# A block of engine programs that ends without GpSimd's drain, in a one-core encoder layer

## The reference

```python
def reference(...):
    for l in range(DEPTH):                      # DEPTH = 1
        xp = mixer_sublayer(xp, ...)            # x + projection of (gated conv, two-way mLSTM)
        xs = mixer_sublayer(xs, ...)
        xp = expert_choice_sublayer(xp, ...)    # 16 experts, each takes its top tokens
        xs = expert_choice_sublayer(xs, ...)
    y_prompt = rms_norm(xp, final_g)
    y_sample = rms_norm(xs, final_g)

def expert_choice_sublayer(x, norm_g, w_router, w_gate, w_up, w_down):
    tokens = rms_norm(x, norm_g).reshape(n_tok, d)
    affinity = softmax(tokens @ w_router)
    gate, idx = lax.top_k(affinity.T, cap)
    xe = tokens[idx]
    hid = silu(xe @ w_gate) * (xe @ w_up)       # per expert
    ye = (hid @ w_down) * gate[..., None]
    out = zeros.at[idx.reshape(-1)].add(ye.reshape(-1, d))
    return x + out
```

## Time and profile before

| | |
|---|---|
| median of three runs | 1306.37 us |
| lowest and highest | 1306.22, 1306.75 us |
| span of the profiled execution | 1307.2 us |
| PE busy in the span | 1253.9 us, 96% |
| POOL busy in the span | 325.7 us, 25% |
| instructions | 25113 |

### The profile page before, as it was taken

One profiled execution on the slowest core, in us unless ns is written; L12 is line 12 of the kernel. 1 busy time (PEld: TensorE's weight loads), 2 busy tenths in 40 slices (PEclk: granted clock), 3 DMA queues, 4 the chain that ended last, 5 costly groups with the idle time before them and its releaser, 6 DMA issues.

```text
span 1307.2 us, 25113 instructions
## 1 busy us (share of the span) xinstructions
PE 1253.9 (96%) x9762; PEld 1029.6 (79%) x9814; DVE 905.7 (69%) x1298; ACT 742.0 (57%) x1079; POOL 325.7 (25%) x316
## 2 busy tenths in 40 slices
PE   7999999999999999779999999999999999999992
PEld 6868986666687888568988898888888888888881
DVE  6462122541586655978888888888888889888985
ACT  7645322222345544447667766776676677667762
POOL 2512221010143231141133213221323132313040
PEclk9999999999999999989999999999999999999996
DMA  8231544361188763388999999999999999999894
GB/s 268 70 116 55 167 140 136 107 180 37 61 256 236 226 211 114 115 312 269 336 305 313 321 334 298 316 324 331 299 310 327 330 298 312 326 331 297 294 372 182
DMA packets 242032, 314.76 MB, mean 241 GB/s; under 512 B 16096, under 2 KB 206048, under 8 KB 241968
## 3 DMA queue, kind: packets, MB, share of 16 engines
q1 hardware_dynamic: 226576, 268.54, 62.2%
q0 software_dynamic: 15392, 45.36, 11.8%
HBM read 274.41 MB, written 39.44 MB: 240 GB/s over the span
## 4 chain that ended last, share of the span: by engine, by line
PE 89%; DMA 4%; DVE 3%; ACT 2%; issue 2%; SPq 1%; POOL 0%; DVEq 0%; ACTq 0%; POOLq 0%
PE psum L2253 23%; PE psum L2114 15%; PE psum L2260 11%; PE psum L2276 8%; PE psum L2081 8%; PE psum L1965 8%; PE psum L2294 4%; PE psum L2285 4%; PE psum L2246 1%; DMA eraw<-in_w_up_dram 1%; PE psum L2027 1%; ACT yt L1248 1%; DMA woraw<-in_w_out_dram 1%; PE psum L1987 1%; PE psum L1945 1%
## 5 line engine op out<-in xcount | busy, mean ns | idle before, releaser
L1812 DVE TENSOR_TENSOR elo<-eraw,ehi 128x2048 bf16<-128x2048 f32 x192 | 433.1, 2283 | 1.0 <-POOLq L822 1.0
L1218 ACT ACTIVATE ehi<-eraw 128x2048 fp32r<-128x2048 f32 x192 | 362.2, 1902 | 25.8 <-PE psum L2294 18.6
L2253 PE MATMUL psum<-xc,ehi 128*128 128x320 f32 x2048 | 332.4, 314 | 1.9 <-DVE xc L1817 1.9
L2253 PEld LDWEIGHTS psum<-xc,ehi 128*128 128x128 f32 x2048 | 304.2, 189 | 3.5 <-DVE xc L1817 2.3
L2260 PE MATMUL psum<-xb,elo 128*128 128x160 bf16 x2048 | 164.4, 234 | 0.0
L1825 DVE TENSOR_REDUCE gu<-psum 128x320 f32<-128x640 f32 x128 | 105.0, 820 | 82.6 <-PE psum L2260 82.5
L2260 PEld LDWEIGHTS psum<-xb,elo 128*128 128x128 bf16 x2048 | 139.0, 98 | 13.2 <-issue 0.2
L2114 PE MATMUL psum<-hn_nar,wnar 128*128 128x512 bf16 (+1 forms) x748 | 141.2, 343 | 1.2
L2276 PE MATMUL psum<-ehi,hc 128*128 128x512 f32 x512 | 132.6, 406 | 0.0
L2114 PEld LDWEIGHTS psum<-hn_nar,wnar 128*128 128x128 bf16 x768 | 73.0, 98 | 63.0 <-issue 4.5
L2276 PEld LDWEIGHTS psum<-ehi,hc 128*128 128x128 f32 x512 | 95.1, 188 | 22.2
(11 more groups left out here) (290 smaller groups left out, 1657.9 us busy)
## 6 DMA issues: line engine op xcount, KB each, us to landing
eraw<-in_w_gate_dram SPq DMA_DIRECT2D x64, 1024.0 KB, 6.3
eraw<-in_w_up_dram SPq DMA_DIRECT2D x64, 1024.0 KB, 8.9
eraw<-in_w_down_dram SPq DMA_DIRECT2D x64, 1024.0 KB, 13.3
wraw<-in_w_in_dram SPq DMA_DIRECT2D x12, 1024.0 KB, 7.5
negm<-negm_d SPq DMA_DIRECT2D x10, 512.0 KB, 7.2
acc_d<-x POOLq DMA_DIRECT2D x10, 512.0 KB, 5.4
tok_d<-tk POOLq DMA_DIRECT2D x10, 512.0 KB, 2.9
v<-v_d SPq DMA_DIRECT2D x18, 256.0 KB, 4.3
```

The source lines that it names most:

```text
L1218: act.activation(f["ehi"][:, j % RING, :], f["eraw"][:, raw_slot(s, j), :], ACT.Copy).then_inc(S["ehi"], 1)
L1812: dve.tensor_tensor(f["elo"][:, j % RING, :], f["eraw"][:, raw_slot(s, j), :], f["ehi"][:, j % RING, :].bitcast(F32), ALU.subtract).then_i ...
L2253: pe.matmul(o[:, 0:2 * NC], hi[:, k, c], x[:, k, :, :].rearrange("p a t -> p (a t)"), start=(k == 0), stop=False, skip_group_check=True)
```

## The change

The block is opened with an argument by which its close has no drain of GpSimd:

```diff
@@ -437,7 +437,7 @@
-        block = out.enter_context(nc.Block())
+        block = out.enter_context(nc.Block(no_gpsimd_drain=True))
 
         @block.sync
         def _(sp):
```

## The result

The changed kernel took 1299.12 us (median of 4 runs, 1297.61 to 1299.81) against 1306.56 us for the kernel before in 4 runs (1306.22 to 1307.04). The ratio is 0.9942, with a 95% interval from 0.9929 to 0.9954. That is 7.4 us less, where 7.75 us were forecast. Five further runs of the changed kernel beside fifteen of the kernel before gave 0.9939 (0.9926 to 0.9953), 1297.91 us against 1306.21 us.

What follows compares the result with a forecast made beforehand. POOL's closing drain, 7.700 us with nothing beside it, was taken to bound the end. Removing it and a 0.05 us step gives 7.75 us: 1306.37 - 7.75 = 1298.62 us, range 1297.7 to 1300.2 us.

Steps and rivals of the forecast that it cites:

- The gap between the last work and the end of the span: From the chain's end at 1296.8 us to 1307.2 us: 10.4 us uncovered, whatever fills it said to lie on the path.
- this landing: Write of line 873, landed at 1299.1 us; claimed to bound the end next, once POOL's 7.700 us drain is gone.
- the step of 0.05 us: At POOL's close, line 150: one instruction-to-instruction step goes with the drain, taken as the middle of nothing and 0.1 us.
- The bounds of the range: Near bounds 1298.5 to 1298.7 us, widened by run spread, span-median difference and a possibly shorter unprofiled drain; chance 0.82.
- The far bounds: Drain size if the profiler caused the long one: 183 ns as POOL's opening drain, or 1.720 us as DVE's closing one.
- the signs that the prediction named: Line 150 without POOL's DRAIN, semaphore instructions at about 1299.3 us, opening DRAIN near 183 ns, line 873 near 1295.8 us.
- Rival A: At the close: the next instruction or launch takes as long, or the argument misses this drain; 1306.4 us, chance 0.08.
- Rival B: Line 2364: the next execution's opening drain walks 176 leftover entries for 7.7 us; 1306.4 us, no change, chance 0.04.
- rival C: Opening drain, line 2364: the uncleared list grows to 352 entries, 15.2 us; 7.3 us slower, 1313.7 us, chance 0.02.
- The estimate of 43 ns for each DMA: POOL's closing drain: (7700 - 183) / 176 DMAs, if it goes through them one by one; the forecast didn't need it.

## Why the prediction was right

**The place.** The gap between the last work and the end of the span was read as path, and was: with the drain gone the end is 3.7 us behind the issue of line 873, which is the 3.4 us of its landing and 0.3 us of close. What is late next is this landing, as said. The run with the drain put back shows the cause, not only the coincidence.

**The size.** 7.700 us of the 7.75 us is the instruction's own duration, and it came back as 7.700 in two experiments with other starts and other spans. From the branch's start to the next semaphore instruction it is 0.2 us in place of 8.0, to a tenth: nothing but the drain went. The runs gave 7.4 us and 8.3 us, each with an interval some 3 us wide that holds 7.75. So they bear out the drain, but can't tell the step of 0.05 us, and that the first of them came within 0.3 us is partly luck. The bounds of the range don't add up as the text says: 0.9 us on each side and a microsecond more above give 1297.6 to 1300.6 us, not 1297.7 to 1300.2 us. Both measured medians lie in either.

**Profiled and not.** The far bounds, from the doubt whether so long a drain is the profiler's doing, weren't needed. The doubt itself isn't settled: every timed run is on record with a span and a clock of its own, so none of them is known to be free of the profiler. And one step was read wrongly. I set the span of 1307.2 us beside the median of 1306.37 us as 0.87 us more. The results give time and span of every run, and the time is 1.7 to 1.8 us over the span: this much lies around it. The profiled execution shown was thus a long one, of some 1308.9 us by this estimate. It did no harm to the forecast, as only a difference was carried over. But it spoiled two of the signs that the prediction named. The last write was to start within a microsecond of 1295.8 us and POOL's two semaphore instructions at about 1299.3 us; they were at 1293.4 and 1296.9 us. A change of over 2 us before 1299 us was to count against the prediction, and there was one, of 2.4 us. What answers it is that kernels with the old close show the same early starts, and that the drain put back brought the old time.

**Rival A** (the time is paid by what comes behind, or the argument reaches another drain) falls by the instruction being absent, its successor starting 0.2 us behind the branch, and the timed runs. **Rival B** (the debt is carried over) and **rival C** (it is carried over and grows) fall by the opening drain of 183 ns and by the times of all nine runs, as far as an execution without the drain went before each. This fits what the Trainium skill says in "Runtime: NRT & Kernel Launch", section "The ~15µs preamble/postamble breakdown", of DMA rings that are reset behind the kernel; no run here shows that reset.

The 12 ns that the Trainium skill gives for boilerplate drains ("VectorE: DVE Perf Modes", section "The DRAIN you can't avoid") are near SP's 7 ns, but not near the other closing ones: 512 ns on PE, 329 ns on ACT and 1720 ns on DVE, and on GpSimd 40 ns with no DMA to go through and 7700 ns here. The page speaks of drains that the runtime puts around a kernel. These stand in the kernel's own program, at the line of its block, so the prediction set the page against a drain that it doesn't describe.

**The estimate of 43 ns for each DMA**, on which the prediction did not rest, was wrong. The price is 75 to 89 ns for each DMA up to 92 at the close, and 82 ns on the average of the 114 in the first expert. Dividing 7.7 us by 176 took it that all 176 were still to be gone through, and the drain's time stands for some 94 of them at this price. Rival C's sum used the same 43 ns and a list that only grows. The closing drain behind 248 DMAs took 4.068 us, so the time doesn't simply grow with the list.

**What stays open.** No run shows why 138 and 176 DMAs cost less than 114. Traffic alone isn't it: all 16 DMA engines were busy throughout the drain behind 114, but also throughout the one behind 174, of which 7.65 us are its own. A list that holds some 94 DMAs, the older ones being struck off while new ones are issued, would give 7.69 and 7.70 us at 138 and 176; but it doesn't give 9.385 us at 114, nor 4.07 us at 248. The other drain that doesn't fit 82 ns for each DMA is the one behind the 38th, with 4.85 us where 3.2 us would be expected; the DMA engines were 13% busy during it. Those behind 60 and 84 lie 0.2 and 0.3 us over it.

## What to carry to other kernels

Compare the end of the last real work with the end of the span. What lies between them is path in full, and a busy-time table or the chain of work shows nothing of it. If the last thing is GpSimd's drain, and the program already waits for the semaphores of all DMAs that GpSimd issued, the drain can go, or be paid earlier: one drain more, at a place where GpSimd idles, took the closing one from 7.7 to 0.2 us. The gain is the closing drain's own time, which the profile shows. Here it was some 80 ns for each DMA that GpSimd issued since its last drain, up to 92 of them, and no more than 7.7 us behind 138 and 176, so a kernel with few DMAs from GpSimd has little to win. Before a drain in mid-kernel is called dear, look whether the engine's own last instruction is still running when it starts.

## What the runs showed of the hardware

- A GpSimd drain at the close, with all data landed, costs 0.040 us with no DMA since the last drain and 0.217, 0.375, 2.677, 5.114 and 7.361 us with 2, 4, 32, 62 and 92. Direct or indirect, 16 rows or 128, 32 packets each or 119, makes no difference that shows.
- It took 9.385 us behind 114 in the first expert, but 7.687 us behind 138 and 7.700 us behind 176 at the close. At 248, of which 72 were small, it was 4.068 us.
- The durations repeat: 7.700 us three times, 2.677 and 9.385 us twice each, in executions whose spans differ by up to 9 us.
- A drain's row starts while GpSimd's instruction ahead of it is still running, and holds what is left of it. Behind four DMAs in the expert loop the row is 0.61 us, of which 0.40 us lie behind the last copy, against 0.375 us at the close.
- Thirty direct DMAs of 128 rows of 16 bytes, 61 KB together, made the span 9 us longer than thirty of 16 rows (1308.7 against 1299.8 us, one run each).
